# Stick-breaking attention: the causal mask is added to the scores in PSUM by DVE instead of by a matmul on PE

## What is computed

```python
causal = s_idx < t_idx
log_beta = jax.nn.log_sigmoid(z)
log_skip_j = jnp.where(causal, jax.nn.log_sigmoid(-z), 0.0)
log_skip = lax.cumsum(log_skip_j, axis=3, reverse=True) - log_skip_j
weights = jnp.where(causal, jnp.exp(log_beta + log_skip), 0.0)
out = einsum('bhts,bhsd->bhtd', weights, v)
```

## Time and profile before

| what | value |
|---|---|
| median of 3 runs | 1241.66 us (1238.97 to 1241.84) |
| profiled execution, its own time | 1240.26 us |
| its span, first to last instruction | 1238.6 us |
| PE busy | 1200.7 us, 97% of the span |
| DVE busy | 767.2 us, 62% |
| ACT busy | 421.6 us, 34% |
| attention of heads 0 to 5 | from 70 us to 457 us of the span |
| attention of heads 6 and 7 | from 457 us to 553 us |

### The profile page before, as it was taken

The page is one execution under the profiler, slowest core; times in us unless marked ns, Lnnn a source line. Parts: engine busy times, 40 slices in busy tenths (PEclk is TensorE's granted clock), DMA queues, the critical chain, the costliest instruction groups (busy, mean ns, idle before and its releaser), DMA issues. The chain is left out here.

```text
span 1238.6 us, 20727 instructions
## 1 busy us (share of the span) xinstructions
PE 1200.7 (97%) x7424; PEld 1099.6 (89%) x7424; DVE 767.2 (62%) x1544; ACT 421.6 (34%) x904; POOL 168.7 (14%) x346
## 2 busy tenths in 40 slices
PE   5999999999999999989989999999999999998998
PEld 5999999999999999878868999999899999897787
DVE  4657485857575767644444676777577777667321
ACT  4545353535353545432232122223222322221210
POOL 2322221212121212100019000000000000000000
PEclk9999999999999999999999999999999999997999
DMA  8210223232312200176522112232323230007542
GB/s 230 60 52 18 69 86 103 85 105 76 105 64 79 67 18 1 48 288 208 177 79 68 35 34 67 89 102 86 96 93 102 86 103 18 17 2 268 197 156 93
DMA packets 112655, 115.56 MB, mean 93 GB/s; under 512 B 6832, under 2 KB 88752, under 8 KB 112560
## 3 DMA queue, kind: packets, MB, share of 16 engines
q1 hardware_dynamic: 112560, 114.32, 28.9%
HBM read 80.75 MB, written 33.55 MB: 92 GB/s over the span
## 5 line engine op out<-in xcount | busy, mean ns | idle before, releaser
L29 PE MATMUL p_proj<-w_qkv_hi,ut_hi 128*128 128x384 f32 x512 | 175.8, 343 | 5.2 <-DVE w_qkv_lo L669 4.3
L31 PE MATMUL p_proj<-w_qkv_hi,ut_lo 128*128 128x384 f32 x512 | 172.4, 337 | 0.0
L30 PE MATMUL p_proj<-w_qkv_lo,ut_hi 128*128 128x384 f32 x512 | 172.1, 336 | 0.0
L29 PE MATMUL p_proj<-g_w_ig_hi,next_hi 128*128 128x256 f32 x512 | 147.2, 288 | 0.0
L31 PE MATMUL p_proj<-g_w_ig_hi,next_lo 128*128 128x256 f32 x512 | 144.4, 282 | 0.0
L30 PE MATMUL p_proj<-g_w_ig_lo,next_hi 128*128 128x256 f32 x512 | 143.9, 281 | 0.0
L29 PE MATMUL p_proj<-next_hi,w_qf_hi 128*128 128x512 f32 x320 | 129.7, 405 | 4.8 <-issue 3.0
L31 PE MATMUL p_proj<-next_hi,w_qf_lo 128*128 128x512 f32 x320 | 126.5, 395 | 0.0
L30 PE MATMUL p_proj<-next_lo,w_qf_hi 128*128 128x512 f32 x320 | 126.3, 395 | 0.0
L699 DVE TENSOR_TENSOR_SCAN a_skip<-a_skip 128x128 f32<-128x128 f32 (+3 forms) x64 | 87.3, 1364 | 33.3 <-ACT a_beta L570 31.2
L29 PEld LDWEIGHTS p_proj<-w_qkv_hi,ut_hi 128*128 128x128 f32 x512 | 96.8, 189 | 6.4 <-issue 4.7
(11 more groups left out here) (185 smaller groups left out, 2738.3 us busy)
## 6 DMA issues: line engine op xcount, KB each, us to landing
stage<-in_sb_w_in_dram SPq DMA_DIRECT2D x32, 512.0 KB, 5.9
stage<-in_hg_w_in_dram SPq DMA_DIRECT2D x32, 512.0 KB, 4.7
w_out_hi_scratch<-m_in SPq DMA_DIRECT2D x32, 256.0 KB, 2.1
w_out_lo_scratch<-m_in SPq DMA_DIRECT2D x32, 256.0 KB, 2.3
m_in<-mixed_scratch SPq DMA_DIRECT2D x12, 512.0 KB, 5.7
a_beta<-in_x_dram SPq DMA_DIRECT2D x8, 512.0 KB, 3.6
mixed_scratch<-a_gated SPq DMA_DIRECT2D x8, 512.0 KB, 3.4
m_in<-in_sb_w_out_dram SPq DMA_DIRECT2D x16, 256.0 KB, 3.2
```

The costliest lines, as they stand in the source:

```text
L29: pe.matmul(out, w_hi, m_hi, start=start, stop=False, skip_group_check=True)
L30: pe.matmul(out, w_hi, m_lo, start=False, stop=False, skip_group_check=True)
L31: return pe.matmul(out, w_lo, m_hi, start=False, stop=stop, skip_group_check=True)
```

## The change

The mask's matmul and its bf16 identity go. DVE adds the mask instead: `mask_scores` waits until all scores of the tile are in PSUM, adds `causal_neg` in place to the last 128 columns of the tile's last unit, and raises a new semaphore `z_masked`. ACT's sigmoids of that last unit wait for `z_masked` where they waited for `z_done`; those of a first of two units still wait for `z_done`. `mask_scores` stands at the head of `weigh` in DVE's program, so directly ahead of the scan of the same tile.

```diff
-            "ident_bf": sb("ident_bf", [P, P], BF16),
...
@@ sigmoids, on ACT
-                    act.wait_ge(z_done, UNITS * h + unit + 1)
+                    if u == Z_UNITS[i] - 1:
+                        act.wait_ge(z_masked, TILES * h + i + 1)
+                    else:
+                        act.wait_ge(z_done, UNITS * h + unit + 1)
...
@@ on DVE
+            def mask_scores(h, i):
+
+                if known_first(h) and i == 0:
+                    dve.wait_ge(pool_made, 6)
+                dve.wait_ge(z_done, UNITS * h + ENDS[i])
+                masked = p_z[(ENDS[i] - 1) % 3][:, (i % 4) * P:(i % 4 + 1) * P]
+                dve.tensor_tensor(masked, masked, c["causal_neg"][:, :], ALU.add).then_inc(z_masked, 1)
+
             def weigh(h, i):
 
+                mask_scores(h, i)
                 width = (i + 1) * P
...
-                        dve.wait_ge(pool_made, 4)
-                        dve.tensor_copy(c["ident_bf"][:, :], c["ident"][:, :]).then_inc(dve_made, 1)
...
@@ scores, on PE
                     pe.matmul(z, qt_hi[b][:, rows], kt_hi[b][:, cols], start=True, stop=False,
                               skip_group_check=True)
-                    if u == Z_UNITS[i] - 1:
-                        pe.matmul(bank[:, width - P:width], c["ident_bf"][:, :],
-                                  c["causal_neg"][:, :], start=False, stop=False, skip_group_check=True)
                     pe.matmul(z, qt_hi[b][:, rows], kt_lo[b][:, cols], start=False, stop=False,
                               skip_group_check=True)
...
@@ step, on PE
                         pe.wait_ge(ut_ready, 2 * TILES)
-                        pe.wait_ge(dve_made, 2)
-                        pe.wait_ge(pool_made, 6)
```

More of the change, by code:

```diff
@@ L369, in build_attention @@
         z_done = sem("z_done")
+        z_masked = sem("z_masked")
         sigmoids_ready = sem("sigmoids_ready")
@@ L638, in step @@
                     if known_first(n) and i == NAT:
-                        act.wait_ge(dve_made, 3)
+                        act.wait_ge(dve_made, 2)
                         act.activation(c["lower"][:, :], c["logit_gap"][:, :], ACT.Sigmoid).then_inc(act_made, 1)
```

## The result

| | before | after |
|---|---|---|
| median of the runs taken side by side | 1240.19 us (20 runs, 1238.64 to 1244.17) | 1244.67 us (20 runs, 1241.02 to 1248.37) |
| ratio, 95% interval | | 1.0037 (1.0028 to 1.0045) |
| span of the profiled execution | 1238.6 us | 1246.2 us |
| PE busy | 1200.7 us, 7424 matmuls | 1198.0 us, 7360 matmuls |

The change costs 0.37%, 4.5 us. The forecast was 1243.3. The profiled execution of the changed kernel is one of its longer ones (1247.91 us), so its span is 7.6 us above before's and not 4.5. I start with the busy time by stretch (columns as in the earlier trace rows); the third line is a short stretch right behind PE's branch at the end of the first pass of the attention loop.

A forecast was written before the change was run, and what follows sets the result against it. PE's issue was taken as the bound, near the end the chain from scores to split. Terms -7.0 + 3.2 + 2.0 + 1.3 + 1.0 + 0.4 gave +0.9, +2.6 with longer hand-offs; +1.7 taken: 1243.3 us, range 1236.5 to 1249.

The forecast's parts named there:

- masks gone from PE: On PE over 8 heads: 64 mask matmuls fewer, 0.12 or 0.08 us each, 0.88 us a head, -7.0 us.
- tile 7, four loop heads: PE's transposes wait for DVE's split of keys, delayed by the mask: 0.8 us a head, +3.2 us.
- tiles 2, 3 of head 6: Masks and sigmoids alternate between DVE and ACT, so PE waits for tile 3's block: +2.0 us.
- tiles 2, 3 of head 7: Same alternation with less before it; PE's fourth transpose waits for the keys' split: +1.3 us.
- rest, and gain swallowed: Other tile pairs and DVE backlogs in heads 6 and 7, 1.0 us; gain lost ahead of two existing waits, 0.4.
- longer hand-off: At some twelve masks on the path, 0.18 us instead of 0.04 per hand-off: up to 1.7 us more.
- rival D: On PE: the removed matmul was partly hidden, so PE gains half, 3.5 us less; 1245.7 us. Chance 5%.
- A: On DVE: overlap is greater than thought, the waits vanish and the removal shows in full; 1235.1 us. Chance 13%.
- B: Loop heads at tile 7 lose more than they gain, DVE lag 1.8 us; 1247.9 us. Chance 20%.
- C: New waits at heads 6 and 7 lower PE's clock, +1.7 to 3.4 us; 1245.1 to 1246.7 us. Chance 12%.

The follow-up runs named there:

- changed kernel with 17 drains: Changed kernel plus 17 drains (instructions that compute nothing) ahead of PE's first wait, moving its code: 1241.0 us, 1.0009 of the kernel before.
- experiment 12: Changed kernel with masks earlier in DVE's order and empty instructions placed so both loop branches are short: 1232.81 us, 0.9944 of the kernel before.
- experiment 11: Kernel before with 97 empty PE instructions, the later 37 in a 4.0 us wait, both loop branches short: 1236.9 us, ratio 0.9973.
- Experiments 3: Kernel before, mask matmul kept on PE, with DVE's mask addition and ACT's wait for it put in besides: 1245.83 us, 1.0045.
- 4: Changed kernel with the masks earlier in DVE's order, PE's code unchanged: 1240.39 us, 0.9997 of the kernel before.
- 8: Changed kernel with 171 empty PE instructions and no causal mask on PE or DVE: 1240.14 us, 1.0004 of the kernel before.
- kernel before with 100 drains: Kernel before with 100 drains (instructions that compute nothing) ahead of PE's first wait, nothing else changed: 1239.17 us, ratio 0.9995.
- earlier masks with 171 drains: Changed kernel with masks earlier in DVE's order and 171 empty instructions in PE's idle stretches at the start: 1241.9 us, 1.0017.

## Why the prediction was right, and where it was wrong

The mechanism that it described held, but its sum missed a term of 3.4 us, three quarters of the loss. That its number was only 1.4 us off is in part luck: it forecast a step of +1.7 us and 4.5 were measured, but it started from a median of three runs, 1241.66, and the 20 runs side by side have 1240.19. The terms are best read where the branches are equal, in the changed kernel with 17 drains against the kernel before: for each PE matmul, its start in the one less its start in the other, as a step at the place where it changes.

| term | predicted | measured |
|---|---|---|
| masks gone from PE | -7.0 | -7.0 if 0.88 a head holds throughout |
| tile 7, four loop heads | +3.2 | +0.69 +0.62 +0.68 +0.63 = +2.6 |
| tiles 2, 3 of head 6 | +2.0 | +1.7 |
| tiles 2, 3 of head 7 | +1.3 | +1.5 |
| rest, and gain swallowed | +1.4 | +1.5, the remainder |
| longer hand-off | 0 to +1.7 | 0, each 0.04 us |
| sum | +0.9 to +2.6, taken +1.7 | +0.3 to the attention's end; +1.1 by the medians |
| code fetch at the branches | not there | about +3.4 |

**The gain on PE was right.** Where no wait disturbs it (experiment 12 against experiment 11, all branches short), PE's lead grows from 8 us to 462 us by 5.48 us, in 6.2 heads: 0.88 us a head, as predicted. Heads 0 and 5 of the changed kernel with 17 drains show it too, 0.88 and 0.89 us each, without a wait of PE. So rival D, a gain half hidden, falls. In heads 6 and 7 some of the lead is lost again: at the attention's end it is 5.7 us, so 1.3 us were swallowed, where 0.4 were taken. Behind the attention these two traces shift against each other by up to 4 us more, now one way and now the other, mostly in how long the clock is at 0.50 near 645 and 1130 us, in stretches where the kernels have the same work; only the medians, 4.1 us, say what is left of the lead.

**The waits were right in place and cause.** The loop heads were slightly over-sized: the lag of 1.06 us was 1.02, and PE's starts fall back by 0.62 to 0.69 us a head, not 0.8 (its idle time there is 0.52). Experiments 3, 4 and 8 show the mechanism from three sides: the waits come with DVE's mask though PE keeps its own, they go when the mask is issued earlier, and they go when it is left out.

**The rivals.** A, the masks hide, is false here, and true of another order: 1232.8 against 1236.9. B needed a mask of 0.35 us and hand-offs of 0.18; they are 0.29 and 0.04, and it is false, though the time came out between the forecast and B's 1247.9. C expected half clock behind the new waits of 1.6 and 1.3 us; the trace shows none near 477 or 526 us. None of the four had a code fetch at a branch, which is what added the rest.

**The step that failed** is the first: "each nanosecond taken from PE's issue shortens the kernel, provided that no other engine becomes late." It took PE's program as a list of instructions whose place has no effect, and so put the branches at nothing. The 4.5 us of loss are 1.1 of the sum and 3.4 of the branches, and the latter is a balance of two: from before to after PE's shift jumps at the attention branch from -0.03 to +7.0 us (4.99 idle, the rest half clock), against which the changed kernel has the HGRN-2 branch free, worth 3.3 us by experiment 11. 7.0 - 3.3 = 3.7, against the 3.4 by the medians (1.0037 less 1.0009). This split of the loss rests on medians that are known to about 1 us either way. The kernel before held the sign of it all along, in a row that the prediction did not ask for: an idle time of 3.03 us with the releaser "issue" at 881.91, behind a loop's branch.

The Trainium skill ("Runtime: NRT & Kernel Launch", section "Instruction fetch mechanics") gives PE a store of 2048 instructions, refilled in blocks of 256 (16 KiB), and says that a taken branch to code outside the window that the engine holds must fetch it first. The trace agrees on the blocks (16 KB a packet) and on the stall, which it shows to be 3.3 to 3.9 us for the branch itself. An estimate from that page: the attention loop's pass, 1669 instructions by the records, is 6.5 blocks of the 8, and the HGRN-2 pass, 1742, is 6.8, so whether both ends fit beside a block fetched ahead depends on where in a block the loop starts: 2048 - 256 - 1669 leaves 123 starts in each 256 at which the attention branch would be short, and 91 in the kernel before, whose loop is 32 longer. The attention branch fits that estimate. In the changed kernel PE stops again 11 instructions behind the start at 1464, so a block would begin at about 1475; the branch is short for starts at 1481, 1513 and 1582 and long at 1464 and 1635, and in the kernel before short at 1481 and 1541 and long at 1581. The same section also speaks of a window of two blocks; for PE no run here bears that out, since branches back over 6.5 and 6.8 blocks were short.

## What to carry to other kernels

Moving a small operation from the bounding engine to an idle one gains near its full price (here 5.7 of 7.0 us to the attention's end) only if it stands in the idle engine's order ahead of that engine's long pieces; look for what stands directly in front of it, and issue the masks of a batch together. In a program with hardware loops as long as these (1669 and 1742 instructions a pass on PE), any change of its instruction count may turn a branch back from short to long: look for idle time with the releaser "issue" behind each branch and for traffic on the instruction queue during the second pass, before and after. Before a change of under 1% is judged, compare at equal branches, by moving the code with instructions in an idle stretch.

## What the runs showed of the hardware that was not expected

- PE's branch back took 0.23 to 0.24 us where the loop's code was held and 3.3 to 3.9 us where not. Behind the long one PE was idle for 1.6 us (kernel before with 100 drains, attention loop) to 5.6 us (earlier masks with 171 drains, HGRN-2 loop), in one stop or in two with some instructions between, and the clock then stood at 0.50, the level of 1.2 GHz, for 3.4 or 6.8 us; behind the stop of 1.6 us it did not fall.
- 17 instructions ahead of a loop moved the whole kernel by 3.5 us; one long branch is worth 3.3 us at the HGRN-2 loop of the kernel before, some 7 us at the attention loop of the changed kernel, where PE stops twice, and 2.7 us (0.9995 less 0.9973) at the attention loop of the kernel before with 100 drains, where PE stops once for 1.6 us and the clock stays up.
- DVE adds to PSUM in place in 290 ns for 128x128, as fast as the same shape read from SBUF (294).
- Where exactly a branch turns long is open by some tens of instructions: in the changed kernel the HGRN-2 branch is short at a start of 7297 and long at 7314, though by the blocks both should be long: 2048 - 256 - 1742 leaves 50 starts, and the second stop with 171 drains puts them from 7476 on, or one block down from 7220 on. The starts at 7491 and 7494 (short) and at 7314, 7346, 7394 and 7468 (long) fit, 7297 alone does not.
